# A two-block transformer kernel: three products a level in the delta rule's inverse, decays and values made beside the gate tiles, and the first norm ahead of the condition

## The reference, cut to what matters

```
mod = (cond @ w_ada[i] + b_ada[i]); sh1, sc1, g1, sh2, sc2, g2 = split(mod, 6)
h = rms_norm(x, norm_g[i, 0]) * (1.0 + sc1) + sh1          # layer 0: the first norm
...
q, k, v = silu(conv(x @ w_in));  q = l2(q) * dk ** -0.5;  k = l2(k)
beta = sigmoid(b);  g = -exp(a_log) * softplus(a + dt_bias);  gam = cumsum(g)
decay = exp(where(i >= j, gam_i - gam_j, -inf))
lower = eye + where(i > j, beta_i * (k_i . k_j) * decay, 0)
delta = lower^-1 (beta * v - carried part)
o = (q_i . k_j) * decay @ delta
o = rms_norm_2(o, norm_w) * silu(z)
```

## Time and profile before

| | |
|---|---|
| time, median of 3 runs | 3236.56 us (3231.42 to 3238.88) |
| profiled execution, own time | 3236.47 us |
| its span | 3234.8 us |
| PE busy | 3014.2 us, 93% of the span |
| DVE busy | 2230.7 us, 69% |
| ACT busy | 1585.7 us, 49% |
| mean granted PE clock | 0.959 of full |

### The profile page before, as it was taken

How to read it: one execution, slowest core, us unless ns; L and a number is a source line. 1 busy time by engine, 2 the same in 40 slices (tenths; PEclk the granted TensorE clock), 3 DMA queues, 4 the chain that set the end, 5 groups by cost and what they waited for, 6 DMA issues and landing times.

```text
span 3234.8 us, 64227 instructions
## 1 busy us (share of the span) xinstructions
PE 3014.2 (93%) x22954; PEld 2896.0 (90%) x22954; DVE 2230.7 (69%) x4709; ACT 1585.7 (49%) x3278; POOL 79.8 (2%) x121
## 2 busy tenths in 40 slices
PE   4997999999999999899999999998997889898898
PEld 4886899999999998799999999998986789886898
DVE  5336479888779974459888867775675358763686
ACT  1110457778544432555777744445442148461574
POOL 2000000000001100000000000001100000000000
PEclk9998999999999998999999999998997899997999
DMA  8520455454478852345444455554330045431453
GB/s 320 221 94 1 149 177 168 152 163 141 156 261 303 300 170 98 124 163 187 153 150 160 141 187 184 186 188 164 120 118 1 14 156 180 163 118 52 143 177 122
DMA packets 137769, 503.50 MB, mean 156 GB/s; under 512 B 15328, under 2 KB 15456, under 8 KB 137344
## 3 DMA queue, kind: packets, MB, share of 16 engines
q1 hardware_dynamic: 122544, 445.57, 41.2%
q0 software_dynamic: 15056, 55.65, 4.8%
HBM read 499.05 MB, written 2.10 MB: 155 GB/s over the span
## 4 chain that ended last, share of the span: by engine, by line
PE 80%; DVE 5%; ACT 4%; issue 1%; DVEq 0%; ACTq 0%
PE PB L509 12%; PE PB L511 12%; PE PB L510 12%; PE PA L509 9%; PE PA L511 9%; PE PA L510 9%; PE PB L499 5%; PE PA L685 4%; DVE w_low L1974 1%; PE PA L885 1%; PE PB L885 1%; PE PA L1025 1%; DVE BIG L2000 1%; PE PA L590 1%; PE PB L582 1%
## 5 line engine op out<-in xcount | busy, mean ns | idle before, releaser
L1062 ACT ACTIVATE w_high<-ring 128x512 fp32r<-128x512 f32 x1484 | 924.4, 630 | 944.3 <-PE PA L511 498.1
L1974 DVE TENSOR_TENSOR w_low<-ring,w_high 128x512 fp32r<-128x512 f32 x1484 | 1014.6, 695 | 430.3 <-ACT w_high L1062 411.9
L509 PE MATMUL PB<-h_high,w_low 128*128 128x256 f32 x3536 | 1024.6, 290 | 44.9 <-DVE h_low L1653 36.9
L511 PE MATMUL PB<-h_high,w_high 128*128 128x256 f32 x3536 | 1003.4, 284 | 0.0
L510 PE MATMUL PB<-h_low,w_high 128*128 128x256 f32 x3536 | 1002.7, 284 | 0.0
L509 PEld LDWEIGHTS PB<-h_high,w_low 128*128 128x128 f32 x3536 | 685.4, 194 | 60.6 <-issue 47.8
L509 PE MATMUL PA<-a_high,w_low 128*128 128x256 f32 x2400 | 678.7, 283 | 10.2 <-DVE a_low L1983 10.1
L511 PE MATMUL PA<-a_high,w_high 128*128 128x256 f32 x2400 | 676.8, 282 | 0.0
L510 PEld LDWEIGHTS PB<-h_low,w_high 128*128 128x128 f32 x3536 | 676.6, 191 | 0.0
L511 PEld LDWEIGHTS PB<-h_high,w_high 128*128 128x128 f32 x3536 | 675.6, 191 | 0.0
L510 PE MATMUL PA<-a_low,w_high 128*128 128x256 f32 x2400 | 674.6, 281 | 0.0
(11 more groups left out here) (326 smaller groups left out, 2849.4 us busy)
## 6 DMA issues: line engine op xcount, KB each, us to landing
ring<-tiles SPq DMA_DIRECT2D x842, 512.0 KB, 3.3
BIG<-ada POOLq DMA_DIRECT2D x96, 512.0 KB, 7.9
BIG<-skew POOLq DMA_DIRECT2D x4, 512.0 KB, 4.5
X<-x SPq DMA_DIRECT2D x1, 1024.0 KB, 5.8
skew<-BIG POOLq DMA_DIRECT2D x1, 1024.0 KB, 6.8
out<-X SPq DMA_DIRECT2D x4, 256.0 KB, 2.0
con<-consts SPq DMA_DIRECT2D x1, 853.0 KB, 8.7
BIG<-masks POOLq DMA_DIRECT2D x1, 768.0 KB, 8.0
```

The lines of the kernel that those rows point to most:

```text
L509: mm(dst, lhs_l, high, start=start, stop=False, skip_group_check=True)
L511: return mm(dst, lhs_h, high, start=False, stop=stop, skip_group_check=True)
L1062: fn(tile_half(w_high, s, b), ring[:, at:at + HALF], ACT.Identity).then_inc(sem("high_ready"), 1)
L1974: tt(tile_half(w_low, s, b), ring[:, at:at + HALF], tile_half(w_high, s, b).bitcast(F32), ALU.subtract).then_inc(sem("low_ready"), 1)
```

## The change: what it does

1. **Start.** PE makes the mean squares before anything of the condition. DVE makes the first group (`ada(0, 1)`), then the norm's reciprocal and scaling, then the second group. PE sums the groups one after the other (8 matmuls each, into PB). ACT waits for `mod_ready` before it modulates.
2. **Condition of the second layer.** 16 of the 48 one-column matmuls stay in the experts. The other 32 stand after the next norm's mean squares; `lru_x` waits for their `mod` after its second tile.
3. **Gates.** `nbeta` goes. PE spreads beta over rows (`beta_rows`, 12 matmuls after tile 3), ACT copies them at j = 4 (`rows`), and DVE makes key decays (decay times beta times strict mask) at j = 9, 12 and 15 and masks the diagonal query decays at j = 11 and 14. It waits once for the attention's table, whose room they take.
4. **Last gate tiles.** The sums of squares run after tiles 38 and 40, the transposes of v after tile 39. ACT scales v and makes the root before it evacuates tile 41.
5. **Pairs.** k is scaled before q. The three key pairs come first, each taken by DVE in one product. The four transposing and scaling steps of the matrix are gone; the six products are ordered so that the inverse starts after the two diagonal key pairs, and the others stand within it.
6. **Inverse.** y is made first and x is its transpose (12 transposes, ACT copies). A level has three products, since `p1` is both the right operand of x's product and the left one of y's. The last level makes y alone. c, p2, n, nt and their mask transfer (`e["low"]`) go.
7. **Tail.** The carried part is subtracted in one operation. The outputs are made in transposed banks in two stages, the first of them before `delta1`; squares are taken from PSUM by ACT and the copy to `mix` is DVE's.

The diff, cut to its core:

```diff
@@ PE: start, second layer's condition
-            ada(0, 2)
+            rms()
+            ada(0, 1, PB, False)
+            ada(1, 2, PB)
             pe.wait_ge(sem("mod_ready"), w.up(sem("mod_ready")))
-            rms()
...
-                    ada(LATER, 12, PB)
+                    ada(LATER, LATER + 2, PB)
...
             rms("experts0")
-            linear("lru_x", H, sem("h_ready"))
+            ada(LATER + 2, 12, PB[:, 1024:])
+            linear("lru_x", H, sem("h_ready"), 0, 2)
+            pe.wait_ge(sem("mod_ready"), w.up(sem("mod_ready"), 2))
+            linear("lru_x", H, None, 2)
@@ PE: even_in
+                    if j == 3:
+                        beta_rows()
...
+                    if j == n - 4:
+                        pe.wait_ge(sem("attention_out_taken"), 4 * TT)
+                        gdn_squares(0)
+                    if j == n - 3:
+                        gdn_values()
+                    if j == n - 2:
+                        gdn_squares(1)
@@ PE: gam_columns
+                    pe.wait_ge(sem("beta_rows_taken"), w.up(sem("beta_rows_taken")))
@@ PE: delta rule
-                for i in range(GDN_HEADS):
+                for i, at in enumerate((3, 4, 5, 0, 1, 2)):
                     if i >= 4:
                         pe.wait_ge(sem("qk_scaled"), i - 3)
-                    spread_roots(2 * GDN_HEADS, 2 * i, (i % 4) * 512)
+                    spread_roots(2 * GDN_HEADS, 2 * at, (i % 4) * 512)
...
+                pe.wait_ge(sem("qk_scaled"), 3)
+                for i in range(3):
+                    pair_products(i)
                 pe.wait_ge(sem("qk_scaled"), w.up(sem("qk_scaled"), GDN_HEADS))
+                pair_products(3)
+                for g in range(2):
+                    pe.wait_ge(sem("inverse_y"), g + 1)
+                    for i in range(6):
+                        ins = nc.tensor.transpose(gdn_bank(g)[:, i * P:(i + 1) * P], block("y", 6 * g + i), ident)
+                    ins.then_inc(sem("inv_p1"), 1)
+                copied = w.up(sem("inv_p1_ready"), 2)
                 for lev in range(1, PAIR_LEVELS):
+                    last = lev == PAIR_LEVELS - 1
                     for g in range(2):
-                        pe.wait_ge(sem("inverse_step"), w.up(sem("inverse_step")))
-                        times(PA, g, "ct", "x").then_inc(sem("inv_p1"), 1)
-                        times(PB, g, "c", "y").then_inc(sem("inv_p2"), 1)
+                        if lev == 1:
+                            pe.wait_ge(sem("inv_p1_ready"), copied - 1 + g)
+                        pe.wait_ge(sem("inverse_x"), 2 * (lev - 1) + g + 1)
+                        times(gdn_bank(g), g, "ct", "x").then_inc(sem("inv_p1"), 1)
+                    if lev == 1:
+                        pair_products(4)
+                        pair_products(5)
                     for g in range(2):
                         pe.wait_ge(sem("inv_p1_ready"), w.up(sem("inv_p1_ready")))
-                        times(PA, g, "y", "p1").then_inc(sem("inv_xpx"), 1)
-                        pe.wait_ge(sem("inv_p2_ready"), w.up(sem("inv_p2_ready")))
-                        times(PB, g, "x", "p2").then_inc(sem("inv_ypy"), 1)
+                        if lev == 1:
+                            pe.wait_ge(sem("pair_taken"), 5 + g)
+                        pe.wait_ge(sem("inverse_y"), 2 * (lev - 1) + g + 1)
+                        if not last:
+                            times(gdn_bank(g), g, "y", "p1").then_inc(sem("inv_xpx"), 1)
+                        times(gdn_bank(2 + g), g, "p1", "y").then_inc(sem("inv_ypy"), 1)
@@ ACT: even_in
                 for j in range(n):
+                    if j == n - 1:
+                        gdn_values()
+                        head_roots(2 * GDN_HEADS, 1.0, GDN_SUMS)
...
+                    if j == 4:
+                        act.wait_ge(sem("gam_psum"), w.up(sem("gam_psum")))
+                        fn(e["rows"], PA[:, 0:12 * P], ACT.Identity).then_inc(sem("beta_rows_taken"), 1)
@@ DVE: even_in
+                    if j == 9:
+                        dve.wait_ge(sem("beta_rows_taken"), w.up(sem("beta_rows_taken")))
+                        dve.wait_ge(sem("gdn_decay"), w.up(sem("gdn_decay"), GDN_HEADS))
+                        dve.wait_ge(sem("swa_table_ready"), 4 * TT)
+                    if j in (9, 12, 15):
+                        key_decay(j // 3 - 3)
+                    if j in (11, 14):
+                        query_decay(j // 3 - 3)
@@ DVE: the order in the delta rule
+                pair_taken(0)
+                pair_taken(1)
+                for g in range(2):
+                    blocks(0, g).then_inc(sem("dve_step"), 1)
+                    dve.wait_ge(sem("dve_step"), w.up(sem("dve_step")))
+                    tt(chunks(gdn_part("y", g), P), over(ident, 6), chunks(gdn_part("ct", g), P), ALU.subtract)\
+                        .then_inc(sem("inverse_y"), 1)
+                for g in range(2):
+                    blocks(1, g).then_inc(sem("inverse_x"), 1)
+                for i in range(2, len(GDN_PAIRS)):
+                    pair_taken(i)
                 for lev in range(1, PAIR_LEVELS):
+                    last = lev == PAIR_LEVELS - 1
+                    for g in range(2):
+                        dve.wait_ge(sem("inv_p1"), w.up(sem("inv_p1")))
+                        if not last:
                             blocks(lev + 1, g)
@@ DVE: start
-            ada(0, 2)
-            modulate(0, 2)
+            ada(0, 1)
             dve.wait_ge(sem("x_loaded"), w.up(sem("x_loaded"), 16))
             rms(None, H)
+            ada(1, 2)
+            modulate(0, 2, PB)
```

More of the change, by code:

```diff
@@ L551, in all_taken, with ada @@
                 pe.wait_ge(taken, q0 + n)
-            def ada(first, last, dst=PA):
+            def ada(first, last, dst=PA, done=True):
                 pe.wait_ge(sem("ada_sums_ready"), last)
@@ L2115, in even_mixer @@
                 inverse_heads(2 * GDN_HEADS)
-                for i in range(GDN_HEADS):
+                for i, at in enumerate((3, 4, 5, 0, 1, 2)):
                     dve.wait_ge(sem("head_scales"), w.up(sem("head_scales")))
-                    x, roots = two(e["qk"], i), two(PA, i % 4)
-                    if i < 3:
+                    x, roots = two(e["qk"], at), two(PA, i % 4)
+                    if at < 3:
                         ins = stt(x, x, float(P) ** -0.5, roots, ALU.mult, ALU.mult)
```

289 lines of the change are left out of this document (138 added, 151 removed).

## The result

The changed kernel takes **3163.86 us** (median of 4 runs, 3163.46 to 3165.24) against 3235.12 us before (median of 4, 3231.42 to 3238.88): a ratio of 0.9778, with a 95% interval from 0.9763 to 0.9794. The prediction was 3163 us in a range of 3154 to 3173. The profiled execution took 3163.46 us, and its span is 73.1 us shorter than that of before. The medians lie 71.3 us apart: the 24 runs of the kernel before lie in two groups, 3230.6 to 3233.7 and 3236.6 to 3239.9 us, and its profile (3236.5) goes with the second.

The account below looks back on a forecast made before the run. PE was taken to bound the kernel, with 80% of the chain that ended last; in the delta rule PE, DVE and ACT bind in turn. The terms sum to -73.6, from 3236.5 to 3163 us, range 3154 to 3173.

Parts of the forecast that it names:

- start: Start of the kernel, mean squares moved ahead of the condition: `hg_in` starts at 48.0 instead of 55.6, -7.6 us.
- condition, 2nd layer: One-column matmuls of the second layer's condition, split between experts and the next norm: -10.1 us, bounds -5 and -11.
- gates: Gates without `nbeta`: ready 1.7 us earlier, -1.7 us, with the added beta rows and decay products hidden.
- last gate tiles: Gate tiles ahead of the spread of roots: PE waits 3.3 us, the clock falls (2.3 us charged); +3.7 us.
- spread to inverse: Delta rule, from first spread of roots to the inverse's first product: 21.1 us instead of 51.4, -30.3 us.
- inverse: Delta rule's inverse, PE-bound, blocks of 1.34 us: 48.3 us instead of 66.8, -18.5 us.
- tail: Delta rule, from the inverse's last block to `even_out`: 23.7 us instead of 32.8, -9.1 us.
- Delta rule: The stretch from the spread of roots through the inverse to `even_out`, forecast as -30.3, -18.5 and -9.1 us.
- The rival of levels bound by their chain: Inverse: ACT's copy or DVE's order holds levels at 10.72 us, five lose 2.7 each; time 3176 us, chance 0.06.
- that of the decays: Gate tiles: DVE's decay products are not hidden, 6.7 us plus 1 us of late beta rows; 3171 us, chance 0.11.
- The rival of the transposes: Delta rule: transposes leave PE's clock low, so level 1 begins at half; 3166 to 3168 us, chance 0.12.
- clock falls in both places: Second layer's condition: clock falls at both blocks of one-column matmuls, saving only 5 us; time 3168 us, chance 0.06.

## Why the prediction was right

The time came out within 1 us of the forecast, inside its range, and by the mechanisms that the forecast named. Part of that closeness is luck, as the terms show. The shift against the kernel before, from stage to stage, in the first trace of the change:

| Term | predicted | measured | read from |
|---|---|---|---|
| start | -7.6 | -7.1 | `hg_in` 55.61 to 48.55 |
| condition, 2nd layer | -10.1 | -6.9 | block to `lru_gates` 67.29 to 60.41 |
| gates | -1.7 | -2.9 | `mixing` to L755/L777 26.30 to 23.45 |
| last gate tiles | +3.7 | +2.9 | spread 14.65 early, convolution's end 17.58 |
| spread to inverse | -30.3 | -30.7 | 51.36 to 20.63 |
| inverse | -18.5 | -18.4 | 66.82 to 48.47 |
| tail | -9.1 | -9.0 | 32.81 to 23.80 |
| other stages | 0 | -0.8 | long stretches, within their scatter |
| sum | -73.6 | -72.7 | `even_out` 2574.63 to 2501.89 |

Each row sets one trace against one, and some stages scatter, so the terms below are also read from the other traces.

**Delta rule (three terms, -57.9).** Right to half a microsecond each in the first trace. The inverse and the tail's path to its sums are as steady as that (60.4 us for both together in twelve traces). From the spread to the inverse it was 20.63 us in the first trace, but 19.05 to 20.90 in ten, median 19.2; by the median the term is -32.2, 1.9 us more than forecast, and that it came within 0.4 is luck. The six DVE operations, the two pair blocks moved in and the blocks of 1.34 us are in the trace as they were counted, and the doubled product shows that PE is the bound in a level, with no slack. The rival of levels bound by their chain falls with it, and that of the decays with the doubled decays (0.8 us for 6.7 us of work). The rival of the transposes falls with the transposes issued eight times.

**Start.** Right. It was 0.5 us less because DVE's first group ended at 28.3 instead of 27.5. The waits for loads inside the group were no longer than before (2.4 and 2.7 us); the whole list began 1.0 us later, since the constants came at 11.53 us instead of 10.54. In the eleven other traces with the new start `hg_in` begins at 47.7 to 48.8 us, median 47.9, and by that the term is -7.7.

**Condition of the second layer.** The direction was right, the size was off: 7 us instead of 10.1, and the condition put back has the same 7.0. The sum had one loss of clock, inside the row of 64, and credited 2.5 us for experts that no longer resume at half. But the clock fell behind the row of 32 too, from 1198.6 to 1202.0 us (half of 3.4 us lost), the row of 64 took 10.86 us instead of 9.3, and together these are 3.3 us, the 3.2 that are missing. The forecast had this as a rival ("clock falls in both places", -5), and its condition came true; only its price was too high, 3.2 us and not 5.1. So the step of the sum that failed is this: one fall of the clock was counted where there were two.

**Gates.** The removed operation is worth what was charged (1.75 us in the run that puts it back). The rest of the 2.9 is the low part ahead of the gates, 2.94 us instead of 4.16, which the forecast doesn't have. It isn't a gain of the change: the first trace is at the lower end of what the same gates do (23.45 us from `mixing` to L777, 23.4 to 27.8 in eleven traces, median 24.3). By the median the term is -2.0.

**Last gate tiles.** The wait of 3.4 us and the fallen clock came as forecast; the cost of the fall was sized at 2.3 us, and the sums show 1.4 (4.12 us instead of 2.76). The run with the sums later shows that this price was for nothing: it was avoidable by one tile.

The errors of +3.2, -1.2, -0.8 and the small ones nearly cancel, so the total looks better than its terms. That the sum came within 1 us is luck; its terms were off by up to 3 us. The sum also starts from a profiled run that is 1.4 us above the median of before (3236.5 against 3235.1).

## What to carry to other kernels

Don't put many one-column matmuls in a row: cut in rows of 16 records between dense tiles they cost their own 0.11 us a record, in rows of 32 to 96 they took TensorE to half clock for 3 to 17 us each, and cutting them gave 6.7 and 4 us in their own stages here. A step that needs the newest result of another engine goes one tile later in a hand-made order if anything dense can stand in front of it; this gave 4 us at once, and in two of three runs 1.5 us or more again through the clock. And when a stage is bound by one engine without slack, count its blocks: the forecast of the inverse came from nothing but the number of blocks times 1.34 us, and was right to 0.2 us.

## What the runs showed of the hardware

- The granted clock fell to half while PE's records were without a gap: PE was busy for all 4.00 us of 1198 to 1202 in the changed kernel, at 0.58, and for 12.00 of 12.00 us from 136 to 148, at 0.57. What had stood before was a row of 32 and one of 64 one-column records. With rows of 16 among dense tiles it stayed at 1.00. The Trainium skill (TensorE: Matmul & The Clock Gate, Part 1) has the clock follow how busy the engine has been; a busy share read from the records doesn't tell it here.
- The fall can come after its cause, when dense work runs again: behind the row of 32 the first split products still had 1.00, and the clock went down 1.4 us after the row's end (0.9 to 1.4 in nine traces).
- Transposes of 128x128 kept the clock at 1.00 for 10.6 us.
- An operation on 12 columns takes 1.72 to 1.77 us on DVE beside POOL's large additions, three times out of three in the kernel before, and 0.17 us (L2086 of the changed kernel) before the additions begin. The low part of a gate tile, two DVE instructions, takes 2.9 to 4.2 us beside them and 1.29 us a tile earlier.
- An unchanged stage of 970 us took 971.5 to 971.9 us in eleven traces and 965.78 in two. In these two the clock from 1300 to 1500 us was 0.95 and 1.00 instead of 0.90 and 0.98, and the stage behind gave back 3 to 4 us of the 6. A single profile of one stage can mislead by as much.
